# The first unit behind three RMS norms multiplies the residual unnormalized; the token's inverse root scales its result

## The chip, the cores and the metric

One NeuronCore of a Trainium2 chip runs the whole program. The metric is device microseconds (us) of one execution, median of several. TensorE (PE) multiplies, VectorE (DVE) and ScalarE (ACT) do the elementwise work, GpSimd (POOL) little, SyncE (SP) issues the loads.

## The reference

Two small transformer blocks over one sequence of 256 tokens with 1024 features, in fp32. What the change touches is the first, of two layers, a convolution mixer and an attention mixer, each followed by an MLP:

```
def rms_norm(x, g):
    y = xf * lax.rsqrt(jnp.mean(xf * xf, axis=-1, keepdims=True) + EPS)
    return (y * g.astype(jnp.float32)).astype(x.dtype)
...
for i in range(DEPTH):
    mod = cond @ ada_w[i] + ada_b[i]
    sh1, sc1, g1, sh2, sc2, g2 = [m[:, None, :] for m in jnp.split(mod, N_MOD, axis=-1)]
    h = rms_norm(x, mix_norm_g[i]) * (1.0 + sc1) + sh1
    y = conformer_conv(h, ...) if i % N_MIXERS == 0 else moba_attention(h, ...)
    x = x + g1 * y
    h = rms_norm(x, mlp_norm_g[i]) * (1.0 + sc2) + sh2
    x = x + g2 * (jnp.square(jax.nn.relu(h @ mlp_w1[i])) @ mlp_w2[i])
```

The norm's factor belongs to the token, so h @ W = r(token) * ((x * gain) @ W) + shift @ W, with gain = g * (1 + sc).

## The kernel before

Features lie on the 128 partitions, in KT = 8 tiles of 256 tokens; X is the residual. Every weight matrix is cut into **units** of 1024 rows by 256 columns (1 MB); the list UNITS fixes their order, and each engine's program is written out by hand as a loop over that list, with a counter semaphore for every hand-over. An engine takes its instructions strictly in the order written. There are no planner and no priorities.

fp32 precision is made from fp32r products: every operand is split into a rounded part (hi) and its remainder (lo). ScalarE rounds a unit's weights into w_hi (split_hi), VectorE subtracts into w_lo (split_lo), each a pass over 128x2048; two units' weights fit (SPLITS = 2), so unit w's split waits until unit w-2 is through TensorE. A unit right behind a norm's first (the dict AHEAD) is split early into F_both, so at a boundary the third unit is the first one whose split must happen there. TensorE either issues three products of 256 columns for each weight tile (three) or, for units in JOINED, one of 512 columns (hi and lo side by side) and one of 256 (joined), whose halves ScalarE and VectorE add later (copy_block, join). Three pairs of PSUM banks take the results (PAIRS = 3).

The modulation vectors (shift, gain, gate) are dot products of a streamed matrix with the condition, done on VectorE (dots, two per chunk) between the splits; the tuple behind MOD_BEFORE says ahead of which unit each chunk stands, VECTORS in which order the vectors come.

Three units open a stage behind an RMS norm: MLP0 = 12 (first MLP), QKV = 44 (attention), MLP1 = 60 (second MLP). At each **boundary**:

1. The last four units of the stage before update X, two tiles each (y and L1369 at MLP0, L1401 at the others); ScalarE squares each tile (squares).
2. TensorE sums the squares over the features with one-column products (early_sums), VectorE and ScalarE make the inverse root (variance, rstd), TensorE spreads it over the partitions (spread_rstd). Dummy products (keep_busy) stand on both sides of the spread.
3. Tile by tile, VectorE multiplies by gain and inverse root (scale_tile), ScalarE adds the shift and rounds (biased_hi), VectorE writes the remainder (L1320). The first unit takes the tiles as they come.

## Time and profile before

| | |
|---|---|
| median of 3 runs | 1205.7 us (1201.86 to 1206.21) |
| span of the profiled execution | 1199.6 us |
| its time by the runs shown | not listed apart; the runs are 2.3 to 6.6 us above its span |
| TensorE busy | 1173.5 us, 98% |
| VectorE, ScalarE busy | 910.5 us, 76%; 598.2 us, 50% |
| three norm boundaries, first sum to third unit | 17.90, 18.25, 17.76 us |

The span runs from the first to the last instruction. A busy share is an average over stages with different limits; TensorE's busy time counts sums, spreads and dummy products too. The time given to an instruction reaches into the next one's, so the distance of starts is the cost of one in a row of many.

### The profile page before, as it was taken

The page shows a single profiled execution, that of the slowest core. Times are in us where ns is not written, and L with a number is a line of the kernel's source. Part 1 is how long each engine was busy: PE and PEld are TensorE (multiplying, and loading weights), DVE is VectorE, ACT ScalarE, POOL GpSimd, SP SyncE. Part 2 cuts the span into 40 slices and gives each one's busy share as a digit, 9 for nine tenths or more (in the row PEclk, how much of TensorE's full clock was granted, in tenths as well). Part 3 has the DMA queues.
Part 4 walks back from the last instruction along what each step waited for, and adds up shares of the span by engine and source line. Part 5 has one row for each costly group of instructions (what it writes and reads, how often), then busy time and mean ns, then how long its engine had stood idle before and what let it go on. Part 6 is the DMA issues. An engine that isn't in the chain of part 4 may idle for free.

```text
span 1199.6 us, 18278 instructions
## 1 busy us (share of the span) xinstructions
PE 1173.5 (98%) x7486; PEld 1006.4 (84%) x7486; DVE 910.5 (76%) x1372; ACT 598.2 (50%) x800; POOL 58.9 (5%) x85
## 2 busy tenths in 40 slices
PE   8998999999999999999999999999999999999997
PEld 6876988888988868899999888888888888898776
DVE  6798788888888677999977664885856676677757
ACT  4597666546544365865465333232212333454873
POOL 0110000000000040000000000000000000000640
PEclk9999999999999999999999999999999999999998
DMA  9994578787768604777765353342444342343000
GB/s 371 333 340 173 211 282 293 281 313 278 278 241 307 225 21 161 266 261 253 275 238 181 141 194 122 140 150 97 152 164 141 110 155 93 125 141 106 2 1 36
DMA packets 34470, 229.48 MB, mean 191 GB/s; under 512 B 4033, under 2 KB 4801, under 8 KB 8146
## 3 DMA queue, kind: packets, MB, share of 16 engines
q1 hardware_dynamic: 33874, 227.14, 52.1%
q0 software_dynamic: 512, 1.16, 0.4%
q8 instruction: 59, 0.97, 0.3%
q14 instruction: 25, 0.20, 0.0%
HBM read 226.08 MB, written 1.05 MB: 189 GB/s over the span
## 4 chain that ended last, share of the span: by engine, by line
PE 83%; DVE 7%; ACT 5%; issue 2%; DMA 2%; SPq 1%; POOL 1%; ACTq 0%; DVEq 0%
PE prod L1900 17%; PE prod L1894 16%; PE prod L1895 15%; PE prod L1896 15%; PE prod L1901 9%; ACT w_hi L641 2%; DMA WS<-first_chunks 2%; DVE w_lo L1083 1%; PE misc L2056 1%; PE misc L2158 1%; PE misc L1809 1%; PE prod L2146 1%; PE misc L1853 1%; PE prod L2133 1%; DVE raw L1116 1%
## 5 line engine op out<-in xcount | busy, mean ns | idle before, releaser
L1083 DVE TENSOR_TENSOR w_lo<-raw,w_hi 128x2048 fp32r<-128x2048 f32 x129 | 295.4, 2290 | 196.4 <-ACT w_hi L641 196.1
L641 ACT ACTIVATE w_hi<-raw 128x2048 fp32r<-128x2048 f32 x129 | 247.1, 1915 | 379.0 <-PE prod L1896 229.0
L1894 PE MATMUL prod<-X_both,w_hi 128*128 128x256 f32 (+1 forms) x656 | 217.7, 332 | 1.6 <-DVE X_both L1320 1.3
L1895 PE MATMUL prod<-X_both,w_hi 128*128 128x256 f32 (+1 forms) x656 | 214.4, 327 | 0.0
L1896 PE MATMUL prod<-X_both,w_lo 128*128 128x256 f32 (+1 forms) x656 | 214.4, 327 | 0.0
L1900 PE MATMUL prod<-X_both,w_hi 128*128 128x512 f32 x592 | 211.3, 401 | 1.8 <-DVE X_both L1320 1.8
L1901 PE MATMUL prod<-X_both,w_lo 128*128 128x256 f32 x592 | 165.8, 280 | 0.0
L1900 PEld LDWEIGHTS prod<-X_both,w_hi 128*128 128x128 f32 x592 | 111.1, 188 | 32.1 <-DVE X_both L1320 3.0
L1894 PEld LDWEIGHTS prod<-X_both,w_hi 128*128 128x128 f32 x656 | 124.5, 190 | 15.6 <-DVE X_both L1320 1.9
L1895 PEld LDWEIGHTS prod<-X_both,w_hi 128*128 128x128 f32 x656 | 124.5, 190 | 10.8 <-issue 0.5
L1896 PEld LDWEIGHTS prod<-X_both,w_lo 128*128 128x128 f32 x656 | 124.5, 190 | 10.7
L1894 PE MATMUL prod<-F_both,w_hi 128*128 128x256 f32 (+1 forms) x384 | 122.8, 320 | 0.2 <-DVE w_lo L1083 0.2
L1896 PE MATMUL prod<-F_both,w_lo 128*128 128x256 f32 (+1 forms) x384 | 122.3, 318 | 0.0
L1895 PE MATMUL prod<-F_both,w_hi 128*128 128x256 f32 (+1 forms) x384 | 122.3, 318 | 0.0
L1901 PEld LDWEIGHTS prod<-X_both,w_lo 128*128 128x128 f32 x592 | 111.7, 189 | 0.0
L1116 DVE CUSTOM_DVE_ANT_0 raw<-raw,cond 128x1024 f32<-128x1024 f32 x80 | 94.0, 1216 | 0.0
L1900 PE MATMUL prod<-F_both,w_hi 128*128 128x512 f32 x256 | 90.5, 398 | 0.0
L1894 PEld LDWEIGHTS prod<-F_both,w_hi 128*128 128x128 f32 x384 | 72.9, 190 | 5.8 <-DVE w_lo L1083 0.6
L1896 PEld LDWEIGHTS prod<-F_both,w_lo 128*128 128x128 f32 x384 | 72.9, 190 | 5.0
L1895 PEld LDWEIGHTS prod<-F_both,w_hi 128*128 128x128 f32 x384 | 72.9, 190 | 4.9
L1901 PE MATMUL prod<-F_both,w_lo 128*128 128x256 f32 x256 | 71.9, 281 | 0.0
L1894 PE MATMUL prod<-w_hi,X_both 128*128 128x256 f32 (+1 forms) x192 | 66.0, 344 | 0.0
(331 smaller groups left out, 1959.5 us busy)
## 6 DMA issues: line engine op xcount, KB each, us to landing
raw<-stream SPq DMA_DIRECT2D x200, 1024.0 KB, 4.9
V<-first_chunks SPq DMA_DIRECT2D x8, 512.0 KB, 12.0
V<-stream SPq DMA_DIRECT2D x2, 1024.0 KB, 17.4
X<-x_features SPq DMA_DIRECT2D x1, 1024.0 KB, 5.2
raw<-first_chunks SPq DMA_DIRECT2D x2, 512.0 KB, 6.4
C<-first_chunks SPq DMA_DIRECT2D x2, 512.0 KB, 17.1
V<-cond_rows SPq DMA_DIRECT2D x1, 1024.0 KB
C<-ctx_features SPq DMA_DIRECT2D x1, 1024.0 KB, 7.1
```

Of the source, the lines that this page charges most:

```text
L641: A(halves(w)[0], places[PLACE[n]].rearrange("p (k c) -> p k c", k=KT), ACT.Copy).then_inc(weight_hi, 1)
L1083: ins = tt(lo, places[PLACE[n]].rearrange("p (k c) -> p k c", k=KT), hi.bitcast(F32), ALU.subtract)
L1116: ins = vec.tensor_tensor_reduce(w, w, cond[:, 0, :], 1.0, 0.0, ALU.mult, ALU.add, got[:, 0, k:k + 1])
L1809: ins = mm(misc[:, bank, c:c + T], ones, src[:, k, :], start=(k == 0), stop=(k == count - 1), skip_group_check=True)
L1853: ins = mm(misc[:, b, 0:1], H[:, k, P * b:P * (b + 1)], ones[:, 0:1], start=(k == 0), stop=(k == KT - 1), skip_group_check=True)
L1894: mm(out, lhs_hi, rhs_hi, start=start, stop=False)
L1895: mm(out, lhs_hi, rhs_lo, start=False, stop=False)
L1896: return mm(out, lhs_lo, rhs_hi, start=False, stop=stop)
L1900: mm(out.rearrange("p (h t) -> p h t", h=2), lhs_hi, rhs, start=start, stop=stop)
L1901: return mm(out[:, 0:T], lhs_lo, rhs[:, 0, :], start=False, stop=stop, skip_group_check=True)
L2056: ins = mm(misc[:, i, P * t:P * (t + 1)], VA[:, t, c:c + P], WS[:, j, :], start=True, stop=True)
L2133: ins = mm(score_pair(p)[:, 512 * off:512 * (off + 1)], q, key, start=(term == 0), stop=(term == 2))
```

## The change

At MLP0, QKV and MLP1 the first unit no longer waits for the norm (PLAIN). ScalarE multiplies each tile of X by the gain as it rounds it, VectorE writes the remainder, both into columns 256 to 511 of X_both; the shift vector goes in as two more columns (both alike), so the unit's products have 258 columns and its result carries shift @ W beside it. VectorE later multiplies the result by the token's inverse root from a copy in rows (scale_plain), and ScalarE adds the shift's share as a bias. The units leave JOINED. The last sums and the spread move into the first unit, the dummy products go, and the second unit is the one that takes the normalized tiles as they come. Vectors are reordered so that gains come before shifts, and the dot products ahead of units 14, 46 and 62 move one or more units later.

```diff
-VECTORS = [(block, layer, part) for block, parts in ((1, 6), (2, 3)) for layer in range(2)
-           for part in range(parts)]
+VECTORS = [(1, layer, part) for layer, parts in ((0, (0, 1, 2, 4, 3, 5)), (1, (1, 0, 2, 4, 3, 5))) for part in parts]
+VECTORS += [(2, layer, part) for layer in range(2) for part in range(3)]
...
-    14, 15, 17, 19,
+    15, 16, 17, 19,
...
-    46, 47, 48, 49, 50, 51, 52, 53,
-    55, 56, 62, 64,
+    47, 48, 49, 50, 51, 52, 53, 54,
+    55, 56, 63, 64,
...
+PLAIN = {MLP0: 2, QKV: 3, MLP1: 4}
...
-KEEP_BUSY = {CONV_OUT: 1, MLP0: 2, QKV: 2, MLP1: 2, MIX_B: 1}
+KEEP_BUSY = {CONV_OUT: 1, MIX_B: 1}
...
+            def plain_tiles_hi(n, k):
+
+                act.wait_ge(mod_step, MOD_DONE[PLAIN_GAIN[n]])
+                act.wait_ge(x_updated, LAST_XU[n] + k + 1)
+                A(XH[:, k, T:2 * T], X[:, k, :], ACT.Copy, scale=mod1[:, GAIN_OF[n], k:k + 1]).then_inc(plain_hi, 1)
...
                 if n in (2, 3, 4):
-                    squares(n, X, H, lambda k: act.wait_ge(x_updated, LAST_XU[n] + k + 1),
-                            (2 * j, 2 * j + 1))
+                    for k in (2 * j, 2 * j + 1):
+                        squares(n, X, H, lambda k: act.wait_ge(x_updated, LAST_XU[n] + k + 1), (k,))
+                        plain_tiles_hi(n, k)
+                    if j == 2:
+                        plain_shift_hi(n)
...
                     biased_hi(i, s, lambda k: mod1[:, shift, k:k + 1])
+                    A(rows[:, 2, :], rs_row(i), ACT.Copy).then_inc(plain_rs, 1)
...
+            def plain_tiles_lo(n, which):
+
+                done = 8 * (n - 2)
+                dve.wait_ge(mod_step, MOD_DONE[PLAIN_GAIN[n]])
+                for k in which:
+                    dve.wait_ge(plain_hi, done + k + 1)
+                    stt(out=XL[:, k, T:2 * T], in0=X[:, k, :], scalar=mod1[:, GAIN_OF[n], k:k + 1],
+                        in1=XH[:, k, T:2 * T].bitcast(F32), op0=ALU.mult, op1=ALU.subtract).then_inc(plain_lo, 1)
...
+            def scale_plain(w):
+
+                n = PLAIN[w]
+                dst = Q[:, 0:2, :] if w == QKV else EV[:, w % 2, :].rearrange("p (i t) -> p i t", i=2)
+                dve.wait_ge(unit_done, w + 1)
+                dve.wait_ge(plain_rs, n - 1)
+                vec.tensor_copy(plain_bias[:, :], tiles(w, T + 2)[:, :, T]).then_inc(plain_scaled, 1)
+                for i in range(2):
+                    ins = tt(dst[:, i, :], tiles(w, T)[:, i, :], rows[:, 2, :], ALU.mult)
+                ins.then_inc(plain_scaled, 1)
...
+                    n = LAST_UPDATE[w][0] if w in LAST_UPDATE and kind != "b_out" else None
+                    if n and j == 3:
+                        plain_tiles_lo(n, (4, 5))
+                        plain_shift_lo(n)
...
+                    if n and j >= 2:
+                        plain_tiles_lo(n, (0, 1, 2, 3) if j == 2 else (6, 7))
...
+                if s - 2 in PLAIN:
+                    scale_plain(s - 2)
...
                 def ready(k):
+                    if w in PLAIN:
+                        n = PLAIN[w]
+                        if k == 0:
+                            pe.wait_ge(shift_lo, n - 1)
+                        if k == 3:
+                            early_sums(n, 3)
+                        if k == 6:
+                            spread_rstd(n)
+                        pe.wait_ge(plain_lo, 8 * (n - 2) + k + 1)
...
+                    c0 = 0
+                    if w in PLAIN:
+                        c0, nt = T, T + 2
...
                 if n in (MLP0, QKV, MLP1):
-                    for j in (2, 3):
-                        early_sums({MLP0: 2, QKV: 3, MLP1: 4}[n], j)
+                    early_sums(PLAIN[n], 2)
```

TensorE at MLP0, before: the last product of unit 11, the sums of squares (misc, from HT), dummy products (from con), the spread (from token_rs), and the first unit.

```order
L1896 MATMUL prod<-X_both,w_lo 128x256
L1853 MATMUL misc<-con,HT 128x1 x12
L1861 MATMUL prod<-con 128x256 x2
L1867 MATMUL misc<-con,token_rs 128x128 x2
L1861 MATMUL prod<-con 128x256 x3
L1900 MATMUL prod<-X_both,w_hi 128x512
```

The same place after the change (the lines of the source have moved; between the pieces stand products of 258 columns like those shown).

```order
L1979 MATMUL prod<-X_both,w_lo 128x256
L1936 MATMUL misc<-con,HT 128x1 x8
L1977 MATMUL prod<-X_both,w_hi 128x258
L1978 MATMUL prod<-X_both,w_hi 128x258
L1979 MATMUL prod<-X_both,w_lo 128x258
...
L1936 MATMUL misc<-con,HT 128x1 x4
...
L1950 MATMUL misc<-con,token_rs 128x128 x2
...
L1983 MATMUL prod<-X_both,F_both 128x512
```

Eight sums stand ahead of unit 12; its 18 products of tiles 0 to 2 come before the last four sums, 18 more before the spread, and 12 behind it; unit 13 (weights in F_both) follows.

VectorE at the same boundary, before: the weights' remainders of units 13 (into F_both) and 12 (w_lo), the updates of X, the inverse root, the tiles, and (ISA) the dot products ahead of unit 14's remainder.

```order
L1083 TENSOR_TENSOR w_lo<-raw,w_hi 128x2048
L1369 TENSOR_TENSOR X<-X,EV 128x256 x4
L1285 TENSOR_SCALAR token_rs<-misc 128x2
L1287 RECIPROCAL token_rs<-token_rs 128x2
L1305 SCALAR_TENSOR_TENSOR HT<-X,mod1,misc 128x256 x2
...
L1320 SCALAR_TENSOR_TENSOR X_both<-HT,mod1,X_both 128x256 x2
L1116 ISA raw,dot<-raw,cond 128x1024
...
L1083 TENSOR_TENSOR w_lo<-raw,w_hi 128x2048
L1344 TENSOR_TENSOR EV<-prod,EV 128x512
```

And after:

```order
L1127 TENSOR_TENSOR w_lo<-raw,w_hi 128x2048
L1442 TENSOR_TENSOR X<-X,EV 128x256 x2
L1386 SCALAR_TENSOR_TENSOR X_both<-X,mod1,X_both 128x256 x6
L1392 TENSOR_TENSOR X_both<-mod1,X_both 128x8x2
L1442 TENSOR_TENSOR X<-X,EV 128x256 x2
L1386 SCALAR_TENSOR_TENSOR X_both<-X,mod1,X_both 128x256 x2
...
L1364 SCALAR_TENSOR_TENSOR X_both<-HT,mod1,X_both 128x256 x2
L1127 TENSOR_TENSOR w_lo<-raw,w_hi 128x2048
L1401 COPY plain_bias<-prod 128x2
L1403 TENSOR_TENSOR EV<-prod,rows 128x256 x2
L1160 ISA raw,dot<-raw,cond 128x1024
```

Six remainders of the unnormalized tiles and the shift's stand between the updates of X's tiles 4, 5 and 6, 7; the eight normalized tiles are still all ahead of unit 14's remainder, from which the dot products are gone.

ScalarE at the same boundary, after the change (before, the rows of X_both from X, of the shift and the copy into rows weren't there):

```order
L1024 ACT_TABLE_LOAD
L788 ACTIVATE EV<-prod,gate_b,mod1 128x256 x2
L663 ACTIVATE HT<-X 128x256
L679 ACTIVATE X_both<-X,mod1 128x256
L684 ACTIVATE X_both<-mod1 128x8x2
...
L673 ACTIVATE token_rs<-token_rs 128x2
L698 ACTIVATE X_both<-HT,mod1 128x256 x8
L952 ACTIVATE rows<-misc 128x256
L656 ACTIVATE w_hi<-raw 128x2048 x2
```

The weight split of unit 14 (w_hi) stands behind all eight roundings, as before, and now behind the copy too.

## Rows read from the trace of the kernel before

**Rows 1.** The page's busy table and its costliest groups (count, busy us, mean ns).

```profile
PE 1173.5 (98%) x7486; PEld 1006.4 (84%) x7486; DVE 910.5 (76%) x1372; ACT 598.2 (50%) x800; POOL 58.9 (5%) x85
...
L1116 DVE CUSTOM_DVE_ANT_0 raw<-raw,cond 128x1024 f32<-128x1024 f32 x80 | 94.0, 1216 | 0.0
```

**Rows 2.** Stretches: length, busy us of PE, PEld, DVE, ACT, POOL; clock; DMA.

```profile
139.26:157.16 17.90, 17.43 (x105) 14.61 (x104) 13.48 (x27) 8.53 (x16) 0.00 (x0) 1.00 0.49 178
328.06:346.31 18.25, 17.43 (x105) 14.62 (x103) 13.11 (x26) 6.99 (x12) 0.00 (x0) 1.00 0.44 169
467.50:485.26 17.76, 17.29 (x104) 14.53 (x103) 12.55 (x25) 9.87 (x15) 0.00 (x0) 1.00 0.45 171
```

**Rows 3.** Timeline of TensorE at MLP0: start, duration, operation, idle before it.

```profile
139.14 0.28 PE L1896 MATMUL prod<-X_both,w_lo 128*128 128x256 f32 x1
139.26 2.74 PE L1853 MATMUL misc<-con,HT 128*128 128x1 f32 x24
...
142.80 0.69 PE L1867 MATMUL misc<-con,token_rs 128*128 128x128 f32 x4
...
145.25 0.50 PE L1900 MATMUL prod<-X_both,w_hi 128*128 128x512 f32 x1 [0.47 <-DVE X_both L1320]
...
157.16 0.40 PE L1900 MATMUL prod<-X_both,w_hi 128*128 128x512 f32 x1
```

**Rows 4.** Timeline of VectorE at MLP0.

```profile
136.07 2.29 DVE L1083 TENSOR_TENSOR w_lo<-raw,w_hi 128x2048 fp32r<-128x2048 f32 x1 [0.19 <-ACT w_hi L641]
138.28 0.75 DVE L1369 TENSOR_TENSOR X<-X,EV 128x256 f32<-128x256 f32 x2
...
144.72 0.48 DVE L1320 SCALAR_TENSOR_TENSOR X_both<-HT,mod,X_both 128x256 fp32r<-128x256 f32 x1 [0.24 <-ACT X_both L671]
...
150.10 0.48 DVE L1320 SCALAR_TENSOR_TENSOR X_both<-HT,mod,X_both 128x256 fp32r<-128x256 f32 x1 [0.18 <-ACT X_both L671]
...
153.71 2.29 DVE L1083 TENSOR_TENSOR w_lo<-raw,w_hi 128x2048 fp32r<-128x2048 f32 x1 [0.83 <-ACT w_hi L641]
```

**Rows 5.** Timeline of ScalarE at MLP0.

```profile
134.04 1.90 ACT L641 ACTIVATE w_hi<-raw 128x2048 fp32r<-128x2048 f32 x1
135.96 1.28 ACT L980 ACT_TABLE_LOAD   x1
137.26 1.02 ACT L759 ACTIVATE EV<-prod,gate_b,mod 128x256 f32<-128x256 f32 x2
...
149.56 0.51 ACT L671 ACTIVATE X_both<-HT,mod 128x256 fp32r<-128x256 f32 x1 [0.28 <-DVE HT L1305]
151.75 1.92 ACT L641 ACTIVATE w_hi<-raw 128x2048 fp32r<-128x2048 f32 x1 [1.68 <-PE prod L1901]
```

**Rows 6.** Timeline of VectorE ahead of QKV.

```profile
323.87 2.29 DVE L1083 TENSOR_TENSOR w_lo<-raw,w_hi 128x2048 fp32r<-128x2048 f32 x1 [0.19 <-ACT w_hi L641]
326.08 1.26 DVE L1401 SCALAR_TENSOR_TENSOR X<-prod,mod,X 128x256 f32<-128x256 f32 x3
```

**Rows 7.** Timeline of VectorE at MLP1.

```profile
465.75 1.26 DVE L1401 SCALAR_TENSOR_TENSOR X<-prod,mod,X 128x256 f32<-128x256 f32 x3
...
485.64 1.23 DVE L1095 TENSOR_TENSOR cond<-V 128x1024 f32<-128x1024 f32 x1 [0.83 <-ACT V L995]
487.90 2.29 DVE L1083 TENSOR_TENSOR w_lo<-raw,w_hi 128x2048 fp32r<-128x2048 f32 x1 [1.03 <-ACT w_hi L641]
```

**Rows 8.** Timeline of TensorE behind the convolution.

```profile
107.83 1.05 PE L1817 MATMUL misc<-con,HT 128*128 128x1 f32 x8 [1.76 <-DVE HT L1240]
```

**Rows 9.** Stretches right behind rows 8, columns as in rows 2.

```profile
110.50:113.00 2.50, 2.50 (x10) 2.14 (x9) 2.28 (x5) 1.96 (x4) 0.00 (x0) 0.50 0.00 0
113.00:114.00 1.00, 1.00 (x4) 0.80 (x3) 1.00 (x4) 0.83 (x3) 0.00 (x0) 0.58 0.00 0
```

**Rows 10.** Timeline of ScalarE at a later norm, where such a copy exists.

```profile
1034.08 0.51 ACT L671 ACTIVATE X_both<-HT,shift 128x256 fp32r<-128x256 f32 x1 [0.28 <-DVE HT L1305]
1034.50 0.36 ACT L935 ACTIVATE rows<-prod 128x256 f32<-128x256 f32 x1
```

More of the change, by code:

```diff
@@ L175 @@
 MOD_DONE = [sum(mod_ops(i) for i in range(vi + 1)) for vi in range(len(VECTORS))]
+PLAIN = {MLP0: 2, QKV: 3, MLP1: 4}
+PLAIN_INDEX = {w: i for i, w in enumerate(PLAIN)}
+PLAIN_GAIN = {2: VEC[1, 0, 4], 3: VEC[1, 1, 1], 4: VEC[1, 1, 4]}
+PLAIN_SHIFT = {2: VEC[1, 0, 3], 3: VEC[1, 1, 0], 4: VEC[1, 1, 3]}
+GAIN_OF = {2: 4, 3: 7, 4: 10}
+SHIFT_OF = {2: 3, 3: 6, 4: 9}
 BY_ACT = {"w1", "q", "k", "v", "a_u", "b_k", "b_v", "b_q"}
@@ L184 @@
 JOINED += [B_OUT, B_OUT + 1, B_OUT + 2]
+JOINED = [w for w in JOINED if w not in PLAIN]
+LATE = JOINED + list(PLAIN)
 ON_X = ("w2", "wo", "b_out")
@@ L219 @@
 LAST = [MLP0 - 1, QKV - 1, MLP1 - 1, MIX_B - 1, NW - 1]
-KEEP_BUSY = {CONV_OUT: 1, MLP0: 2, QKV: 2, MLP1: 2, MIX_B: 1}
+KEEP_BUSY = {CONV_OUT: 1, MIX_B: 1}
 FIRST_MEAN = {1: 4, 5: 6, 7: 6}
 BY_TOKEN = (0, 1, 2, 3, 4, 5, 7)
-SPREAD_IN = {CONV_OUT: (1, 6), MLP0: (2, 3), QKV: (3, 3), MLP1: (4, 3), MIX_B: (5, 3)}
+SPREAD_IN = {CONV_OUT: (1, 6), MIX_B: (5, 3)}
 LAST_UPDATE = {}
@@ L776, in drain @@
                     dst, sq = (Q, H) if kind == "q" else (K1, C)
-                    if w not in JOINED:
-                        A(dst[:, 2 * j:2 * j + 2, :], tiles(w, T), ACT.Copy)
-                    A(sq[:, 2 * j:2 * j + 2, :], dst[:, 2 * j:2 * j + 2, :] if w in JOINED else tiles(w, T),
-                      ACT.Square).then_inc(drained["act"], 1)
+                    if w in PLAIN:
+                        for i in range(2):
+                            A(sq[:, i, :], dst[:, i, :], ACT.Square, bias=plain_bias[:, i:i + 1])
+                            ins = A(dst[:, i, :], dst[:, i, :], ACT.Identity, bias=plain_bias[:, i:i + 1])
+                        ins.then_inc(drained["act"], 1)
+                    else:
+                        if w not in JOINED:
+                            A(dst[:, 2 * j:2 * j + 2, :], tiles(w, T), ACT.Copy)
+                        A(sq[:, 2 * j:2 * j + 2, :], dst[:, 2 * j:2 * j + 2, :] if w in JOINED else tiles(w, T),
+                          ACT.Square).then_inc(drained["act"], 1)
                 elif kind == "v":
@@ L982, in _ @@
                     copy_block(s - 2)
-                if s - 3 in JOINED and UNITS[s - 3][0] not in ("w2", "b_out"):
+                if s - 3 in LATE and UNITS[s - 3][0] not in ("w2", "b_out"):
                     drain(s - 3)
-                if s >= 2 and s - 2 not in JOINED and s - 1 != A_OUT_2 and UNITS[s - 2][0] != "conv_g":
+                if s >= 2 and s - 2 not in LATE and s - 1 != A_OUT_2 and UNITS[s - 2][0] != "conv_g":
                     drain(s - 2)
@@ L1367, in drain @@
                         k = 2 * j + i
+                        if j == 3 and i == 0:
+                            plain_tiles_lo(2, (4, 5))
+                            plain_shift_lo(2)
                         dve.wait_ge(y_ready, k + 1)
@@ L1743, in _ @@
                     join(s - 2)
-                if s - 3 in JOINED and UNITS[s - 3][0] == "w1":
+                if s - 2 in PLAIN:
+                    scale_plain(s - 2)
+                if s - 3 in LATE and UNITS[s - 3][0] == "w1":
                     drain(s - 3)
-                if s >= 2 and not early and (s - 2 not in JOINED or UNITS[s - 2][0] != "w1"):
+                if s >= 2 and not early and (s - 2 not in LATE or UNITS[s - 2][0] != "w1"):
                     drain(s - 2)
```

33 lines of the change are left out of this document (29 added, 4 removed).

## The prediction

> **What bounds the kernel now.** The first view is the page's busy table: TensorE is busy for 1173.5 of 1199.6 us [rows 1], so a change pays only where TensorE stands still or does work that isn't products. The second is the table of stretches. Each of the three is one boundary behind an RMS norm, from the first sum of squares after the last unit of the stage before to the first product of the third unit of the new stage: 17.90, 18.25 and 17.76 us [rows 2]. Two units of 5.65 us are useful there (the unit in the middle of the first stretch ends at 157.16, and ScalarE's wait that ended at 151.75 was for the unit before it [rows 3, 5]). So 6.5 us are lost at each boundary, 19.7 us in all, and that is the most that the change can win.
>
> The third view is TensorE's timeline at MLP0 [rows 3]: sums of squares from 139.26, the spread of the inverse root at 142.80 (call its start S), the first product at 145.25, the third unit at 157.16. The fourth is VectorE's and ScalarE's: from S the eight tiles are scaled, rounded and split, one every 0.78 us, until VectorE begins the last remainder at 150.10 = S + 7.3 [rows 4]. ScalarE begins its last rounding at 149.56 = S + 6.76, then waits 1.68 us for TensorE to release a weight buffer and splits the third unit's weights at 151.75 [rows 5]; VectorE follows at 153.71 and is done at 156.00 [rows 4], 1.16 us before TensorE wants them. **So two slacks, 1.68 us on ScalarE and 1.16 us behind it, separate the norm's chain from the third unit.** What matters is where the third unit begins.
>
> **What the change does to it.** Unit one is taken off the norm, but units two and after still need normalized tiles, and the same 8-tile chain runs once the spread is done. The spread now stands inside unit one, ahead of its seventh tile, with the last sums ahead of the fourth. Hence for each boundary
>
> S' = start of unit one + 6 tiles x 6 products x 0.12 us + 4 sums. The step 0.12 is that between the last product and the first sum [rows 3]; 258 columns for 256 add under 1%. A third of the 24 sum records in 2.74 us is 0.91 us. Together S' = start + 5.23 us. The inverse root itself is ready in time: from the sums' end at 142.0 to S were 0.8 us, and it now has three tiles, 2.16 us.
>
> From S' the third unit follows by the chain alone: last rounding begins at S' + 6.76; the new copy of the row of inverse roots begins 0.4 us later and takes 0.36 us (the same copy at a later norm [rows 10]), so the weight split starts at S' + 7.5, takes 1.92 us [rows 5], and VectorE's half 2.29 us [rows 4]: **third unit at S' + 11.8 us**. The middle unit, paced by the remainders, is over at S' + 8.7 (145.25 - 142.80 = 2.45, and 6.25 for eight tiles), so TensorE then stands idle for 3.1 us. The removed dot products (two of 1.22 us [rows 1]) give nothing here: VectorE had to wait 0.83 us for ScalarE behind them [rows 4].
>
> When does unit one start? It needs the sums of two blocks (1.82 us after the last product) and, on VectorE, the tiles 4 and 5 of X, then six remainders (0.40 us each, the distance of starts of such operations; the row's 0.48 overlaps the next) and the shift's small one (I take 0.15, as no such shape has a row; ends 0.1 and 0.5): 2.55 us.
> - MLP0: ScalarE is busy without a pause ahead of it, so the two gain multiplications added to the block before (0.4 us each) move the weight split of 134.04 by 0.8 us [rows 5]; VectorE's half, which waited for it, goes from 136.07 to 136.87, and X's tiles 4 and 5 from 138.28 to 139.1 [rows 4], done 139.9. Unit one starts at 142.45 (the sums end at 141.08), S' = 147.7, third unit 159.5 against 157.16: **+2.3 us**.
> - QKV: the same shift, VectorE's half from 323.87 to 324.65, which it awaited for 0.19 us, and the tiles from 326.08 to 326.9 [rows 6], done 327.7; unit one at 330.3, S' = 335.5, third unit 347.3 against 346.31 [rows 2]: **+1.0 us**.
> - MLP1: no shift, tiles 4 and 5 from 465.75 [rows 7], the remainders done by 469.1, sums by 469.32; S' = 474.55, third unit 486.35 against 485.26 [rows 2]: **+1.1 us**.
> - MLP1, fourth unit: VectorE's queue between the third unit's weights (S' + 11.75) and the fourth's now holds the scaling of unit one (1.0 us: two passes over PSUM of 0.42, as three such took 1.26 [rows 6], and a tiny copy), the SiLU product of 1.23, two dot products 2.3 and the split 2.25: ready at S' + 18.55, wanted at S' + 17.45: **+1.1 us**. Before, the split at 487.90 ended 0.7 us ahead of need (485.26 + 5.65) [rows 7].
>
> At MLP0 and QKV the same count without the SiLU product gives S' + 17.2, hidden by 0.25 us. Unit one itself is 48 products of 0.12 = 5.8 us against 5.65 and lies in S' already. The reordered vectors leave each gain and shift ready before its use, for they keep their chunks. Sum: 2.3 + 1.0 + 1.1 + 1.1 = **+5.5 us**. On the profiled execution's span that is 1199.6 + 5.5 = 1205.1; the median of before lies 6.1 us above that span (launch and end lie around it; the lowest run is 2.3 above), so 1211.2, say 1211.
>
> **The clock.** The change drops the dummy products ahead of unit one and opens idle gaps. The case's own rows: behind the convolution TensorE had been idle 1.76 us and then did one-column products; the granted clock was 0.50, its lower level of 1.2 GHz, from 110.5 and 0.58 in the slice from 113 [rows 8, 9]. That cost 0.5 x 2.5 + 0.42 x 1 = 1.7 us. At the norms of rows 2 it stayed at 1.00 with idle pieces of 0.5 to 0.9 us.
>
> **The rivals.**
> - *The clock falls in the new gaps* (3.1 us with nothing, ahead of each third unit). For it: a shorter pause did it [rows 8, 9]. Against: there weak work went on both sides, while here dense products stand up to the gap. Three falls at 1.7 us: 1211 + 5 = 1216. Chance 0.17. The Trainium skill (TensorE: Matmul & The Clock Gate, "Why this matters for your kernels") warns of idle gaps between bursts, after which the clock returns to the low level; the rows of the convolution agree in kind, and no row here has a gap like the new one.
> - *VectorE falls behind* after the boundary, since dot products now stand in three units in a row (15, 16 and 17; before 14, 15 and 17). Each such unit needs 0.6 + 0.6 + 2.3 + 2.25 = 5.75 us of VectorE against 5.65; it decides once 0.25 us of cover is gone. Price 0.3 to 0.6 us at each boundary: 1212.5. Chance 0.13.
> - *Faster: the third unit's weights don't wait.* If the split came free by S' + 8.7 (3.1 us sooner than the rows say, the point from which it decides), the third units start at 156.4, 344.2 and 483.25, that is 0.8, 2.1 and 2.0 us earlier, and no SiLU wait: 1205.7 - 4.9 = 1200.8. For it: rows 5 show ScalarE's wait was for TensorE, not for the norm. Against: ScalarE and VectorE take their orders in turn, the split stands behind the eighth tile, and no row is shorter. Chance 0.13, with all that would make my chain too long.
> - *No change that matters*: the starts of unit one come 0.8 us sooner than I have them and the copy hides: 1208. It is the low end of my own case.
>
> **How the numbers follow.** My case has 0.53, own range 1208 to 1213.5; clock 0.17, VectorE 0.13, faster 0.13, unforeseen 0.04. The bounds of the small prices (0.1 to 0.5 for the shift, 0.25 of cover, 0.8 us of shift at two places) move the sum by 3 us; the range 1204 to 1217 holds all but most of the faster rival and the clock's far end. A measurement tells no change from one of 0.5%, 6.0 us here, so 1211 lies just within it and cases are cut at 1211.7: my case splits 0.30 same, 0.23 slower; the clock and most of VectorE's are slower; of the faster rival 0.09 are more than 0.5%. Together faster 0.10, same 0.42, slower 0.48.
>
> **What would show it.** TensorE's timeline: unit one's first product 3.2, 2.2 and 1.9 us after the first sum, the spread 8.4, 7.4 and 7.1 us after it; the third unit 11.8 us behind the spread, with an idle of some 3 us released by VectorE's weight remainder, a wait that before hardly had a row. ScalarE's split of the third unit's weights should follow the row copy without a pause. The boundary stretches should measure 20.2, 19.2 and 18.9 us. I am wrong if the split starts before the eighth rounding is done, if the spread stands earlier than 5 us behind unit one's start, or if the granted clock leaves 1.00 there.

## The result, and the profile after

| | median | runs | span of the profiled execution | its mean granted clock |
|---|---|---|---|---|
| before | 1203.78 us | 1200.68 to 1206.21 (4) | 1199.6 us | 0.996 |
| changed | 1223.72 us | 1219.93 to 1224.53 (4) | 1221.2 us (time 1222.97) | 0.987 |

The change makes the kernel slower: ratio 1.016, 95% interval 1.0142 to 1.0177. I had forecast 1211.0, range 1204 to 1217, and slower with 0.48.

The stretches of the changed kernel that answer to [rows 2], from the first sum of squares to the third unit; then, inside the first of them, unit one up to the spread and the rest:

```profile
138.82:163.53 24.71, 19.98 (x110) 18.08 (x108) 14.21 (x35) 12.68 (x25) 0.00 (x0) 0.79 0.23 86
333.55:358.07 24.52, 19.86 (x111) 18.07 (x109) 14.12 (x34) 11.68 (x22) 0.00 (x0) 0.79 0.23 86
478.74:497.74 19.00, 15.51 (x110) 13.80 (x109) 12.70 (x31) 10.70 (x20) 0.00 (x0) 1.00 0.25 104
142.40:151.88 9.48, 9.48 (x44) 9.48 (x45) 1.71 (x6) 1.72 (x5) 0.00 (x0) 0.51 0.35 143
151.88:163.53 11.65, 8.35 (x50) 6.66 (x48) 8.92 (x19) 8.32 (x12) 0.00 (x0) 1.00 0.01 1
```

Forecast were 20.2, 19.2 and 18.9. The third came as forecast; in the first two the granted clock (the number behind the five engines) is 0.79 in the mean, and 0.51 while unit one runs. TensorE's timeline at MLP0, for [rows 3]:

```profile
138.82 2.35 PE L1936 MATMUL misc<-con,HT 128*128 128x1 f32 x16
142.40 0.55 PE L1977 MATMUL prod<-X_both,w_hi 128*128 128x258 f32 x1 [1.24 <-DVE X_both L1392]
142.75 0.42 PE L1978 MATMUL prod<-X_both,w_hi 128*128 128x258 f32 x1
142.97 0.42 PE L1979 MATMUL prod<-X_both,w_lo 128*128 128x258 f32 x1
...
151.88 0.61 PE L1950 MATMUL misc<-con,token_rs 128*128 128x128 f32 x4
...
154.35 0.47 PE L1983 MATMUL prod<-X_both,F_both 128*128 128x512 f32 x1 [0.44 <-DVE X_both L1364]
...
163.53 0.50 PE L1983 MATMUL prod<-X_both,w_hi 128*128 128x512 f32 x1 [2.87 <-DVE w_lo L1127]
```

The clock had fallen before unit one began. The sums of squares end at 141.17; a third of a microsecond later, from 141.50, the clock is at 0.50, while TensorE still waits for the shift's remainder:

```profile
141.50:142.40 0.90, 0.00 (x0) 0.03 (x1) 0.90 (x5) 0.41 (x1) 0.00 (x0) 0.50 1.03 437
```

Unit one starts at 142.40 (forecast 142.45), but its products follow each other every 0.215 us instead of 0.12, though nothing is waited for. The spread therefore comes at 151.88 and not at 147.7. Behind the spread all goes as forecast: the third unit 11.65 us after the spread (forecast 11.8), with an idle of 2.87 us (forecast 3.1) released by VectorE's remainder. ScalarE and VectorE there, for [rows 5] and [rows 4]:

```profile
158.57 0.51 ACT L698 ACTIVATE X_both<-HT,mod 128x256 fp32r<-128x256 f32 x1 [0.28 <-DVE HT L1349]
158.99 0.36 ACT L952 ACTIVATE rows<-misc 128x256 f32<-128x256 f32 x1
159.25 3.70 ACT L656 ACTIVATE w_hi<-raw 128x2048 fp32r<-128x2048 f32 x2
```

```profile
159.12 0.48 DVE L1364 SCALAR_TENSOR_TENSOR X_both<-HT,mod,X_both 128x256 fp32r<-128x256 f32 x1 [0.18 <-ACT X_both L698]
161.19 2.29 DVE L1127 TENSOR_TENSOR w_lo<-raw,w_hi 128x2048 fp32r<-128x2048 f32 x1 [1.59 <-ACT w_hi L656]
```

Last rounding, row copy, weight split and weight remainder stand one behind the other, in the predicted order. In the table of TensorE's waits (us in total, times, longest) the first row is this wait, for the three third units and the fourth unit at MLP1:

```profile
PE prod L1983 <- DVE w_lo L1127: 9.5, 4, 2.9
```

That is not the whole loss. A copy on ScalarE ahead of the recurrence stage, which runs once, is a landmark in the middle of the program. From the view of one source line, before and after:

```profile
L927 ACT ACTIVATE EV<-misc x1: 1007/1007/1007, 660.3 to 660.3; 128x1024 f32<-128x1024 f32 x1
```

```profile
L971 ACT ACTIVATE EV<-misc x1: 1005/1005/1005, 674.0 to 674.0; 128x1024 f32<-128x1024 f32 x1
```

Up to it 13.7 us are lost. From it to the end before takes 1199.6 - 660.3 = 539.3 us and after 1221.2 - 674.0 = 547.2: **7.9 us are lost in code that the change doesn't touch**. From 680 to 980 us TensorE is busy without a gap at clock 1.00 in both kernels. Its groups there, before and then after (count | busy, mean ns):

```profile
L1894 PE MATMUL prod<-X_both,w_hi 128*128 128x512 f32 x256 | 100.2, 391 | 0.0
L1895 PE MATMUL prod<-X_both,w_hi 128*128 128x512 f32 x256 | 99.6, 389 | 0.0
...
L1895 PE MATMUL prod<-F_both,w_hi 128*128 128x512 f32 x69 | 26.8, 389 | 0.0
...
L1894 PE MATMUL prod<-w_hi,X_both 128*128 128x512 f32 x64 | 24.9, 389 | 0.0
```

```profile
L1977 PE MATMUL prod<-X_both,w_hi 128*128 128x512 f32 x234 | 92.6, 396 | 0.0
...
L1978 PE MATMUL prod<-X_both,w_hi 128*128 128x512 f32 x233 | 91.7, 393 | 0.0
L1977 PE MATMUL prod<-w_hi,X_both 128*128 128x512 f32 x84 | 33.1, 394 | 0.0
...
L1978 PE MATMUL prod<-F_both,w_hi 128*128 128x512 f32 x64 | 25.3, 395 | 0.0
```

Each of these products takes 2 to 6 ns more. The distance of their starts is what they cost in a row: it was 0.227 us before (27 steps from 859.82 to 865.94 in TensorE's timeline) and is 0.232 us after (26 steps from 859.79 to 865.83). Behind the landmark the kernel before has 1575 records of such products that read `X_both` or `F_both`; 0.005 us each would be 7.9 us, an estimate that meets the loss. What they share with the change is the buffer `X_both`, whose rows grew from 512 to 514 elements (2048 to 2056 bytes), so that `F_both`, allocated behind it, moved by 128 bytes.

### The profile page after: what moved, and what is told of

Its sections match the earlier page's. It is cut to its first block, busy times and chain, and to the rows that moved or that the text cites. A ratio compares the mean times of both kernels' runs of the same rounds, so it can differ in the third digit from the quotient of the medians.

```text
span 1221.2 us, 18417 instructions
## 1 busy us (share of the span) xinstructions
PE 1182.4 (97%) x7504; PEld 1011.9 (83%) x7504; DVE 920.9 (75%) x1405; ACT 608.0 (50%) x832; POOL 58.9 (5%) x85
## 4 chain that ended last, share of the span: by engine, by line
PE 78%; DVE 10%; ACT 6%; issue 3%; DMA 2%; SPq 1%; POOL 1%; ACTq 0%; DVEq 0%
PE prod L1977 15%; PE prod L1979 15%; PE prod L1978 15%; PE prod L1983 14%; PE prod L1984 7%; ACT w_hi L656 2%; DVE w_lo L1127 2%; DMA BS<-first_chunks 2%; PE misc L2151 1%; DVE HT L1349 1%; DVE raw L1160 1%; PE misc L2253 1%; PE misc L1892 1%; PE prod L2241 1%; DVE X_both L1364 1%
## 5 line engine op out<-in xcount | busy, mean ns | idle before, releaser
L1977 PE MATMUL prod<-X_both,w_hi 128*128 128x256 f32 (+2 forms) x704 | 235.7, 335 | 4.4 <-DVE X_both L1392 2.5
L1979 PE MATMUL prod<-X_both,w_lo 128*128 128x256 f32 (+2 forms) x704 | 232.0, 330 | 0.0
L1978 PE MATMUL prod<-X_both,w_hi 128*128 128x256 f32 (+2 forms) x704 | 231.6, 329 | 0.0
L1983 PE MATMUL prod<-X_both,w_hi 128*128 128x512 f32 x544 | 192.8, 397 | 9.5 <-DVE w_lo L1127 9.5
L1984 PE MATMUL prod<-X_both,w_lo 128*128 128x256 f32 x544 | 152.7, 281 | 0.0
L1977 PEld LDWEIGHTS prod<-X_both,w_hi 128*128 128x128 f32 x704 | 135.8, 193 | 19.6 <-issue 3.7
L1978 PEld LDWEIGHTS prod<-X_both,w_hi 128*128 128x128 f32 x704 | 136.3, 194 | 12.3 <-issue 0.4
L1979 PEld LDWEIGHTS prod<-X_both,w_lo 128*128 128x128 f32 x704 | 136.1, 193 | 11.8
L1983 PEld LDWEIGHTS prod<-X_both,w_hi 128*128 128x128 f32 x544 | 102.5, 188 | 35.7 <-DVE w_lo L1127 11.1
L1984 PEld LDWEIGHTS prod<-X_both,w_lo 128*128 128x128 f32 x544 | 102.7, 189 | 0.0
```

The costliest lines, as they stand in the source:

```text
L1977: mm(out, lhs_hi, rhs_hi, start=start, stop=False)
L1978: mm(out, lhs_hi, rhs_lo, start=False, stop=False)
L1979: return mm(out, lhs_lo, rhs_hi, start=False, stop=stop)
L1983: mm(out.rearrange("p (h t) -> p h t", h=2), lhs_hi, rhs, start=start, stop=stop)
L1984: return mm(out[:, 0:T], lhs_lo, rhs[:, 0, :], start=False, stop=stop, skip_group_check=True)
```

## The experiments

There are three theories for the 20 us: the chain behind the spread (forecast), the clock at unit one, and the place of the operands in memory. Two columns of the profile tell them apart: the time of the landmark copy ("ahead"), which holds the three boundaries, and the span behind it ("behind"). Each is from the one profiled execution of a kernel; medians and ratios are from all its runs, always against the kernel before on the same chip. "Ahead" swings by up to 5 us with each fall of the clock that the one execution happened to have: e12 had one at each of the three boundaries, e14 one at MLP0, e3 short ones at MLP0 and QKV, and the profile of before none there. "Behind" hardly swings.

| kernel | median | ratio to before, 95% interval | ahead | behind |
|---|---|---|---|---|
| before | 1203.0 to 1204.9 | | 660.3 | 539.3 |
| changed | 1223.72 | 1.0160 (1.0142 to 1.0177) | 674.0 | 547.2 |
| e1_filled | 1219.30 | 1.0125 (1.0096 to 1.0154) | 670.3 | 547.1 |
| e2_bare | 1207.91 | 1.0035 (1.0019 to 1.0050) | 668.9 | 540.1 |
| e3_wide | 1210.99 | 1.0055 (1.0036 to 1.0075) | 660.1 | 547.5 |
| e4_early | 1215.60 | 1.0096 (1.0071 to 1.0121) | 669.2 | 548.3 |
| e5_pad | 1206.00 | 1.0014 (1.0005 to 1.0024) | 661.1 | 542.1 |
| e6_rows8 | 1209.31 | 1.0049 (1.0032 to 1.0066) | 658.8 | 546.5 |
| e7_after8 | 1224.35 | 1.0166 (1.0146 to 1.0186) | 675.8 | 546.6 |
| e8_early8 | 1214.05 | 1.0091 (1.0072 to 1.0110) | 666.1 | 546.0 |
| e9_pieces | 1207.46 | 1.0025 (1.0011 to 1.0039) | 659.9 | 546.1 |
| e10_apart | 1219.57 | 1.0125 (1.0106 to 1.0144) | 678.2 | 539.3 |
| e11_all | 1223.39 | 1.0147 (1.0124 to 1.0170) | 682.2 | 539.4 |
| e12_pad256 | 1204.73 | 1.0005 (0.9989 to 1.0021) | 664.3 | 539.7 |
| e13_inrow | 1219.15 | 1.0127 (1.0106 to 1.0148) | 678.1 | 539.3 |
| e14_inrow_all | 1205.70 | 1.0010 (0.9998 to 1.0023) | 664.1 | 540.0 |
| e15_one_dummy | 1209.43 | 1.0039 (1.0022 to 1.0055) | 668.8 | 539.6 |
| e16_three | 1204.04 | 0.9993 (0.9983 to 1.0004) | 660.8 | 539.8 |
| e17_dots | 1206.44 | 1.0018 (1.0009 to 1.0028) | 664.9 | 539.7 |

### The clock: e1_filled and e2_bare

```diff
 e1_filled, against the changed kernel
-KEEP_BUSY = {CONV_OUT: 1, MIX_B: 1}
+KEEP_BUSY = {CONV_OUT: 1, MLP0: 2, QKV: 2, MLP1: 2, MIX_B: 1}
 e2_bare, against the kernel before
-KEEP_BUSY = {CONV_OUT: 1, MLP0: 2, QKV: 2, MLP1: 2, MIX_B: 1}
+KEEP_BUSY = {CONV_OUT: 1, MIX_B: 1}
-SPREAD_IN = {CONV_OUT: (1, 6), MLP0: (2, 3), QKV: (3, 3), MLP1: (4, 3), MIX_B: (5, 3)}
+SPREAD_IN = {CONV_OUT: (1, 6), MLP0: (2, 0), QKV: (3, 0), MLP1: (4, 0), MIX_B: (5, 3)}
```

> The changed kernel with the two dummy products ahead of unit one put back at MLP0, QKV and MLP1 (they fall into the 1.2 us in which TensorE waits for the shift's remainder). Theory: the granted clock fell to 0.50 because the dummies are gone. Then it stays at 1.00 at MLP0 and QKV, the two stretches from first sum to third unit come to 19 to 20 us instead of 24.7 and 24.5, and the time to 1223.7 - 9.8 = about 1214. Rival: the one-column sums inside unit one or the waits make it fall whatever stands before: 0.50 stays for some 10 us and the time is 1223 to 1225.

> The kernel before without its dummy products at MLP0, QKV and MLP1 (two ahead of the spread and three behind it at each). Theory of the clock: the granted clock falls to 0.50 at one to three of the boundaries, at 4 to 5 us each, so 1208 to 1218. Rival, the dummies count for nothing here and only the changed order brought the fall: within 2 us of the kernel before, clock 1.00 throughout the boundaries.

With the dummies back the stretches are:

```profile
138.97:160.51 21.54, 18.10 (x115) 15.90 (x113) 14.16 (x35) 12.62 (x25) 0.00 (x0) 0.92 0.26 99
332.06:352.20 20.14, 16.68 (x114) 14.47 (x112) 14.11 (x34) 11.68 (x22) 0.00 (x0) 1.00 0.27 105
474.45:493.97 19.52, 16.21 (x115) 14.44 (x113) 12.71 (x31) 10.71 (x20) 0.00 (x0) 1.00 0.25 102
```

At QKV the fall is gone and 4.4 us with it; at MLP0 it is still there, but shorter (0.50 from 141.3 to 144.7), and the stretch is 3.2 us less. The median gained 4.4 us and not the 9.8 expected, and with four runs each the intervals of the two ratios overlap, so e1 alone would be weak evidence. Slices of 2 us show why: in e1 the clock falls at MLP0 and QKV right *behind* the third unit's wait of 2.9 us (0.70, 0.50, 0.95 from 161 us; 0.50, 0.66 from 353 us), where the changed kernel's profile shows no fall. So the clock can fall at that wait too, in some executions. Taking the dummies out of the kernel before costs 4.9 us in the median, and in the profile the clock falls at all three boundaries (0.57 in the mean from 146 to 153 us). Its ratio has an interval that lies above 1, so the rival, that the dummies count for nothing in the old order, falls. The dummies don't rule a fall out, though: e12, the kernel before with a small unused buffer and all its dummies, has one at each boundary in its profile (0.57 in the mean from 142 to 150 us) and the median of before.

### The place of the operands: e3_wide, e5_pad, e6_rows8, e12_pad256, e7_after8

```diff
 e3_wide; e6_rows8 has + 8; e7_after8 is the changed kernel with + 8 for + 2
-        X_both = sb("X_both", [P, 2, KT, 2 * T], F32R)
+        X_both = sb("X_both", [P, 2, KT, 2 * T + 2], F32R)
 e5_pad; e12_pad256 has [P, 64]
         X_both = sb("X_both", [P, 2, KT, 2 * T], F32R)
+        shifted = sb("shifted", [P, 32])
```

> The kernel before with the rows of X_both two columns longer (514 for 512 elements) and nothing else: the extra columns are never written or read. In the changed kernel some 7 us went missing between 670 and 986 us, in products whose mean was 394 ns against 389, without a wait and at clock 1.00. Theory of the rows (stride or place of the buffers in memory): products of the recurrence stage take 394 ns here as well and the time is about 1211. Rival, pace is of the run or of the program's instructions, not of the buffer: 389 ns and 1203 to 1206.

> The kernel before with an unused buffer of 128 bytes a partition behind X_both, which moves every later buffer as the wider rows did but leaves the rows of X_both at 2048 bytes. Theory of the rows' stride: products stay at 389 ns in the recurrence stage and the time within 2 us of the kernel before (1203). Rival, place of the later buffers: 394 ns and about 1211.

> The kernel before with rows of X_both eight elements longer (2080 bytes, a multiple of 32) instead of two (2056, a multiple of 8). Theory A, a row must begin at a multiple of 32 bytes or less: 389 ns and about 1203. Theory B, it wants 64 or the old power of two: 394 ns, about 1211.

> The changed kernel with rows of X_both eight elements longer instead of two, nothing else. If e6 keeps 389 ns, this takes the 7 us of pace off the changed kernel and leaves its waits and its clock: 1223.7 - 7.5 = about 1216. If rows of 2080 bytes are as slow as those of 2056: 1223 to 1224.

> The kernel before with an unused buffer of 256 bytes behind X_both (e5 had 128). In e5 the products on F_both took 395 ns and those on X_both 389; in e6 F_both lay 512 bytes further and took 389. If 256 bytes are a good step: F_both at 389 ns, the time of the kernel before. If not: 395 ns and some 2 us more, as e5.

e3 adds columns that nothing reads or writes, and loses 8.2 us behind the landmark and in sum none ahead of it, though its profile has two short falls of the clock there. That is the untouched code's whole loss. The groups of e3, then of e5, from 680 to 980 us:

```profile
L1895 PE MATMUL prod<-X_both,w_hi 128*128 128x512 f32 x251 | 98.7, 393 | 0.0
...
L1895 PE MATMUL prod<-F_both,w_hi 128*128 128x512 f32 x64 | 25.3, 395 | 0.0
...
L1894 PE MATMUL prod<-w_hi,X_both 128*128 128x512 f32 x64 | 25.2, 394 | 0.0
```

```profile
L1896 PE MATMUL prod<-X_both,w_hi 128*128 128x512 f32 x256 | 99.6, 389 | 0.0
...
L1896 PE MATMUL prod<-F_both,w_hi 128*128 128x512 f32 x66 | 26.0, 394 | 0.0
...
L1895 PE MATMUL prod<-w_hi,X_both 128*128 128x512 f32 x65 | 25.3, 389 | 0.0
```

In e5, `X_both` keeps its rows and its products their 389 ns, and only the moved `F_both` is slow; so the place matters operand by operand. The third row of each is the value stage, where the moving operand `w_hi` (allocated ahead of `X_both`) hasn't moved and the stationary one is a piece of `X_both`: with the wider rows it costs 394 as well.

e6 (rows of 2080 bytes, `F_both` 512 bytes further) has `X_both` at 393 to 397 and `F_both` at 389 to 391. e12 (256 bytes) has all at 389 to 391 and the time of before. So rows longer by 8 or 32 bytes and a shift of 128 bytes cost 4 to 6 ns a product in most groups, shifts of 256 and 512 nothing. e7 followed: no gain, as e6 had said by then.

Why does the loss stand behind the landmark alone, though the stages ahead of it multiply from the same two buffers? Ahead of it a unit's products have 256 columns, or the unit is joined, and then a product's 512 columns are two pieces of 256, hi and lo, and not one row of 512. These products didn't get slower. From 160 to 320 us, before and then e3:

```profile
L1900 PE MATMUL prod<-X_both,w_hi 128*128 128x512 f32 x217 | 76.8, 399 | 0.0
```

```profile
L1900 PE MATMUL prod<-X_both,w_hi 128*128 128x512 f32 x219 | 77.2, 396 | 0.0
```

On `F_both` they took 399 ns before and 393 in e3, and the products of 256 columns 281 ns against 281 to 283. So the cost is that of products whose 512 moving columns are one piece.

### The chain: e4_early, e8_early8, e9_pieces

```diff
 e4_early: e1 and
-                        if k == 3:
+                        if k == 2:
                             early_sums(n, 3)
-                        if k == 6:
+                        if k == 4:
                             spread_rstd(n)
 e8_early8: e4 with rows of 2 * T + 8
 e9_pieces: e8 and, on ScalarE behind the spread (its split_hi for that unit taken out)
+                    for k in range(KT):
+                        biased_hi(i, s, lambda k: mod1[:, shift, k:k + 1], which=(k,))
+                        q = k - 3
+                        if q == 0:
+                            act.wait_ge(slot_loaded[PLACE[WHERE[u]]], 16 * LOADS[WHERE[u]])
+                            act.wait_ge(unit_done, u - 1)
+                        if 0 <= q < 4:
+                            ins = A(halves(u)[0][:, 2 * q:2 * q + 2, :], place[:, 2 * q:2 * q + 2, :], ACT.Copy)
```

> The changed kernel with the two dummy products back and, inside unit one, the last tiles' sums one tile earlier (ahead of tile 2 instead of 3) and the spread of the inverse root two tiles earlier (ahead of tile 4 instead of 6). Theory of the chain: the third unit starts 11.7 us behind the spread; the spread comes 1.4 us earlier if the root is there in time, so TensorE's 2.9 us wait ahead of each third unit shrinks to about 1.5 and the time is some 4.3 us below that with the dummies alone, about 1210. Rival: the third unit's weights wait for something other than the spread, the wait stays 2.9 us and the time is that with the dummies alone.

> The changed kernel with the two dummy products back, the last sums one tile earlier, the spread two tiles earlier, and rows eight elements longer. If the losses add: 1215.6 - 7.5 = about 1208, still 5 above the kernel before, for the rest of the waits ahead of the third units (about 1.5 us at three places). If rows of 2080 bytes are slow too: 1215 to 1216.

> The kernel e8 (dummies, earlier sums and spread, rows eight elements longer), and ScalarE rounds the third unit's weights in four pieces between the roundings of tiles 3 to 7 instead of in one piece behind all eight and the copy of the row; the copy stands last. Theory: the chain behind the spread (eight tiles on VectorE and ScalarE, then ScalarE's 1.9 us, then VectorE's 2.3 us) holds the third unit; VectorE's weight remainder then follows its last tile without the 1.6 us pause, the wait of 2.56 us ahead of each third unit falls to 1.0 to 1.4, and the time is 3.5 to 4.8 us below e8, some 1210. Rival: the third unit waits for its weights' transfer or for unit two; the wait and the time of e8 (1214) stay.

e4 gained 3.7 us on e1, near the 4.3 expected (the intervals of the two ratios overlap), but not as I had written it: the wait ahead of the third unit stayed at 2.5 us. At MLP1 the spread stands at 481.31 and the third unit starts at 492.96, again 11.65 us later. Unit two moves with the spread as well, so an earlier spread shortens the stretch and leaves the wait. e8 missed its 1208 by 6 us because rows of 2080 bytes are slow. e9 cuts the chain itself:

```profile
140.65:158.28 17.63, 16.24 (x114) 14.49 (x112) 14.18 (x35) 11.28 (x26) 0.00 (x0) 1.00 0.33 120
328.66:346.00 17.34, 16.04 (x115) 14.43 (x113) 14.00 (x34) 10.38 (x24) 0.00 (x0) 1.00 0.33 122
466.50:483.42 16.92, 15.68 (x115) 14.43 (x113) 12.83 (x31) 10.69 (x23) 0.00 (x0) 1.00 0.29 118
```

VectorE's remainder follows its last tile without a pause, the wait is 1.24 us, and no fall of the clock is left at a boundary. It is 6.6 us faster than e8, more than the 3.5 to 4.8 expected: the three stretches give 56.47 - 51.89 = 4.6 us, and e8's profile had falls behind the third unit's wait (0.71 and 0.50 from 349 us, 0.70 and 0.50 from 489 us) that the shorter wait doesn't bring.

### The shift's columns elsewhere: e10_apart, e11_all, e13_inrow

```diff
 e10_apart, against the changed kernel (e11_all: the same on e4 with e9's pieces)
-        X_both = sb("X_both", [P, 2, KT, 2 * T + 2], F32R)
+        X_both = sb("X_both", [P, 2, KT, 2 * T], F32R)
...
+        shift_both = sb("shift_both", [P, 2, KT, 2], F32R)
...
+                            mm(out, a, hi_k, start=(k == 0), stop=False, skip_group_check=True)
+                            mm(out, a, lo_k, start=False, stop=False, skip_group_check=True)
+                            ins = mm(out, b, hi_k, start=False, stop=(k == KT - 1), skip_group_check=True)
 e13_inrow, against the changed kernel
+                act.wait_ge(unit_done, {2: MLP0, 3: QKV, 4: MLP1}[n])
-                A(XH[:, :, 2 * T:2 * T + 2], mod1[:, SHIFT_OF[n], :].unsqueeze(2).broadcast_to([P, KT, 2]),
+                A(XH[:, :, T - 2:T], mod1[:, SHIFT_OF[n], :].unsqueeze(2).broadcast_to([P, KT, 2]),
...
-                        c0, nt = T, T + 2
+                        c0, nt = T - 2, T + 2
```

> The changed kernel with the rows of X_both back at 512 elements: the shift's two columns lie in a buffer of their own at the end of the memory, and unit one multiplies them in 48 products of two columns of its own behind its last tile; its eight tiles are products of 256 columns and no longer wait for the shift. Theory of the rows: products of the recurrence stage are back at 389 ns, 7.5 us less, and 1.2 us of wait less at MLP0 and QKV; the 48 products take 3 to 6 us at each boundary, of which what lies beside the chain that holds the third unit is free: 1214 to 1217. Rival, the pace comes from anything else in the changed kernel: 394 ns and 1221 to 1225.

> All together: the shift in a buffer of its own as in e10, the dummies, the earlier sums and spread, and the third unit's weights in pieces. If every loss is understood: 1215.6 (e4) - 7.5 (rows) - 4 (pieces) = 1204, give or take 2 for the 48 small products and the shift's wait: no different from the kernel before, or a little faster. If something in the changed order costs by itself, 1208 or more.

> The changed kernel with the shift's two columns in the last two places of each row's first half, written when the unit ahead has been multiplied, so that unit one still multiplies 258 columns in one piece and the rows of X_both are 512 elements again; ScalarE waits for unit one's end ahead of its fifth rounded tile. No dummies, sums and spread as in the changed kernel. Theory of the rows: 389 ns in the recurrence stage and 1223.7 - 7.5 = 1216, or somewhat less where the shift's wait of 1.2 us goes. Rival: 394 ns, 1222 to 1225.

In all three the span behind the landmark is back at 539.3 to 539.4 us: in the changed kernel too, the rows alone made the 7.9 us. But ahead of it all three are worse than the changed kernel, and e10's median, 1219.57, lies above its 1214 to 1217. Two of e10's 48 small products at QKV and the stretches at MLP0 (sums to their start; the small products; behind them):

```profile
342.08 0.25 PE L2107 MATMUL prod<-shift_both,w_hi 128*128 128x2 f32 x1
342.20 0.25 PE L2108 MATMUL prod<-shift_both,w_hi 128*128 128x2 f32 x1
```

```profile
139.39:148.64 9.25, 9.15 (x79) 9.04 (x77) 5.92 (x18) 4.86 (x14) 0.00 (x0) 1.00 0.60 229
148.64:156.24 7.60, 7.60 (x50) 7.60 (x49) 5.65 (x14) 3.64 (x8) 0.00 (x0) 0.68 0.00 0
156.24:163.00 6.76, 6.76 (x26) 5.81 (x27) 4.58 (x7) 1.91 (x1) 0.00 (x0) 0.60 0.19 45
```

A product of two columns, each with new weights, is followed by the next after 0.11 us, as one of 256 columns is after 0.12, and while 48 of them run the clock falls: it is at 1.00 for the first 2.7 us at MLP0 and 4.0 us at QKV, and at 0.50 for the rest. e11 was expected at 1204 and came to 1223.39; the small products were priced at 3 to 6 us in e10 and 2 in e11, and neither text thought of the clock. e13 keeps the two columns in the same products. Its median was expected at 1216 and is 1219.15: the shift can be written only when the unit ahead has been multiplied, so unit one waits longer for it (1.91, 2.02 and 0.78 us, where the changed kernel had 1.24, 1.23 and none), and its profile has falls at all three boundaries.

### All causes away: e14_inrow_all, e15_one_dummy, e16_three, e17_dots

```diff
 e14_inrow_all: e13's columns, e1's dummies, e4's sums and spread, e9's pieces
 e15_one_dummy: e14 with MLP0: 1, QKV: 1, MLP1: 1
 e16_three: e14 with MLP0: 3, QKV: 3, MLP1: 2
 e17_dots: e16 and, in the table,
-    55, 56, 63, 64,
+    55, 56, 62, 64,
```

> e9 with the columns inside rows of 512 elements as in e13. If the causes are the rows, the clock and the chain: 1207.5 (e9) less 5 to 6 for the products on X_both, 1201.5 to 1203, a little faster than the kernel before (1204). If the changed order costs something else as well, 1205 or more.

> e14 with one dummy product ahead of unit one at the three boundaries instead of two. If one holds the clock, 0.4 us less at each, 1.2 us in all. If the clock falls with one, 3 to 8 us more than e14.

> e14 with three dummy products instead of two at MLP0 and QKV, where TensorE still waits 0.7 and 0.8 us for the shift; the third lies in that wait. If the gap is what fells the clock there: 0.50 no more at MLP0 and QKV, median 1203 or below (e14 was 1205.7). If the clock falls by chance of where the sums lie: 1205 to 1206, as e14.

> e16 with the table's row for MLP1 as in the kernel before (a weight row's dot products ahead of unit 62 instead of 63). Theory: the wait of 0.73 us ahead of the fourth unit of MLP1 is VectorE's remainder being late behind the dot products that the moved row put there; with the row back it is gone and the time 0.7 us below e16, hardly to be told by the time but by the wait. Rival: the fourth unit waits because the table load and the conditioning's SiLU stand on ScalarE ahead of its weights; the wait stays.

e14 takes back 18 of the 20 us and stands 2.7 us above the upper end of its expectation. One fall at MLP0 is in its profile. It began at 142.1, while the dummies still ran, just ahead of the shift's wait of 0.7 us (142.30 to 143.02), so that wait alone didn't bring it. One dummy less costs 3.7 us (expected 3 to 8 if the clock falls). A third one, in the shift's wait, leaves no fall at the boundaries in its one profile and gives 1204.04. e14's and e16's intervals overlap, so that the third dummy did it is not shown. Expected was 1203 or below; the profiled execution has the span 1200.6. Against the kernel before the ratio is 0.9993 (0.9983 to 1.0004), which is no difference. Its three stretches are 18.06, 18.06 and 16.92 us, in sum 53.0 against 53.9 before, and the fourth unit at MLP1 waits 0.83 us: next to nothing is left. That is the best version of the change that I found.

e17 fell out against its theory. With the dot products ahead of unit 62 they stand between VectorE's last tile and the third unit's remainder (two of 1.22 us), so the fourth unit's wait is gone, as expected, but the third unit waits much longer. From the timelines of TensorE in e16 and e17:

```profile
484.25 0.50 PE L1997 MATMUL prod<-X_both,w_hi 128*128 128x512 f32 x1 [1.22 <-DVE w_lo L1139]
490.90 0.50 PE L1997 MATMUL prod<-X_both,w_hi 128*128 128x512 f32 x1 [0.83 <-DVE w_lo L1139]
```

```profile
486.79 0.80 PE L1997 MATMUL prod<-X_both,w_hi 128*128 128x512 f32 x1 [3.52 <-DVE w_lo L1139]
```

2.3 us more there against 0.83 less. And the clock fell in that longer wait; behind it TensorE ran at 0.50 (the first product's 0.80 us, against 0.50 us in e16, shows it too), where e16's profile has no fall:

```profile
486.79:492.40 5.61, 5.61 (x17) 4.84 (x18) 5.58 (x8) 2.88 (x6) 0.00 (x0) 0.50 1.02 432
```

Here the intervals of the ratios (1.0009 to 1.0028 against 0.9983 to 1.0004) are apart. The table's new row was the better one.

## Why the prediction was wrong

- **The chain** held. Unit one's start (142.45; measured 142.40), the chain from spread to third unit (11.8; 11.65 at all three), TensorE's idle ahead of it (3.1; 2.87 to 2.89), the order of ScalarE's and VectorE's work, and the stretch at MLP1 (18.9; 19.00) came as worked out. The wait of the fourth unit at MLP1 (1.1) is 0.90. e9 shows that this chain is the cause of the wait. Of the smaller sums two are slightly off: the loss at the boundaries of before is 53.9 less six units of 5.65, that is 20.0 us, not 19.7, and "S' + 17.2" adds up to 17.3, which leaves 0.13 us of cover instead of 0.25; neither is in the +5.5 us.
- **The sum's step "S' = start of unit one + 6 tiles x 6 products x 0.12 us + 4 sums" failed at MLP0 and QKV**, because 0.12 us is the distance at clock 1.00. Measured was 0.215, S' - start was 9.48 us instead of 5.23, and the stretches 24.71 and 24.52 instead of 20.2 and 19.2: 9.8 us in the profiled execution. I had the clock as a rival (0.17), and as a sign of being wrong, but in the wrong place and at 1.7 us a fall: I looked at the gap ahead of the third unit and gave the dropped dummies ahead of unit one no price. There the two things stand together that the convolution's rows have, a pause and one-column products (here 2.35 us of sums, then a wait of 1.24 us), and the clock was down 0.3 us into the wait. A fall cost 4.9 us, because it lasted through all of unit one. e2 (+4.9 us) and e15 (+3.7 us) show that fewer dummies cost time there, with more or longer falls in their profiles, and e1 fits; that the dummies keep every fall away is not shown (e1 and e12 have some in spite of them). e1 and e13 show falls in or behind the third unit's wait as well, so the rival's own gap is not innocent. By the rule cited with it from the Trainium skill (TensorE: Matmul & The Clock Gate, "Why this matters for your kernels"), idle gaps between bursts bring the lower level back; the traces agree in kind, but here the clock fell after 0.3 us of idle behind the sums, while at 2.87 us between dense products it fell in some executions and not in others.
- **A term was missing**: the two columns were counted only in the products that read them ("258 columns for 256 add under 1%"). Widening the buffer's rows cost 7.9 us in the products that read 512 columns in one piece from it or from its neighbour, hundreds of microseconds away from the change; the joined products and those of 256 columns show no such cost. e3 measures it alone (+8.2 us behind the landmark), e5, e6 and e12 show which operand pays, and e10 and e13 show it in the changed kernel.
- **The other rivals**: VectorE behind in three units in a row shows no wait at MLP0 and QKV; the remainder's four waits are those of the chain. The faster case would have needed the third unit's weights sooner; e9 made that so by another order on ScalarE, and with it the stretches (51.9 us in sum) are shorter than those of before (53.9).
- **The account**: 13.7 us ahead of the landmark are 14.3 in the three stretches and 0.9 at the fourth unit, less 1.5 that came back between them, which no run here takes apart; 7.9 us lie behind it. Of the 14.3, 9.8 are the clock and 4.5 the chain, which was forecast as 4.4. This is measured against a profile of before that has no fall at these boundaries (mean clock 0.996; other executions of that kernel have 0.984 to 0.996), so the share of the clock in the medians, 19.9 us apart, can be smaller. In the medians the change costs 19.9 us (1223.72 - 1203.78), where +5.5 was forecast; the forecast stood on an earlier median of before, 1205.7. How the clock's share varies from run to run isn't known from one profile: the other runs of the changed kernel had a mean clock of 0.986 to 0.991.

## What to carry to other kernels

Before a buffer is widened or a small one added, look at what lies behind it: here longer rows of one matmul operand, and the shift of the next one by 128 bytes, made products of 512 columns in one piece 2% slower (0.232 us for 0.227) in code that nobody touched. Leave such rows and addresses where they are, and put additions behind the operands, or into columns that are free at that time. When a reordering takes filler work out of the way, ask what stood beside it: here one-column sums and a wait, around which the clock fell and stayed down for as long as ten microseconds of dense work. And a unit that is freed from a chain gives nothing while the next one still waits for the whole chain. Splitting the weights in pieces between the tiles shortened that wait from 2.56 to 1.24 us; with all other causes away too, the moved unit came out even with the kernel before and not ahead of it.
